# Filler matmuls in the last down product, one combine at its end, and another order of the final norm

## The reference

```python
h2 = rms_norm(x, norm_ffn[l])
for e in range(N_EXPERTS):                       # 32 experts, two chosen per token
    a = jax.nn.silu(hf @ w_gate[e]) * (hf @ w_up[e])
    out = out + combine[:, e:e + 1] * (a @ w_down[e]).astype(f32)
x = x + out
return rms_norm(x, norm_final)                   # y = x * rsqrt(mean(x*x) + EPS) * g
```

## Time and profile before

| | us |
|---|---|
| runs | 728.23, 729.10, 728.98 |
| profiled execution, its own time | 728.23 |
| its span | 726.3 |
| TensorE busy (matmul) | 554.2 (76%) |
| DVE, ACT, POOL busy | 204.1, 72.6, 43.9 |
| weights and other reads | 240.86 MB |

### The profile page before, as it was taken

How to read it: one execution, slowest core, us unless ns; L and a number is a source line. 1 busy time by engine, 2 the same in 40 slices (tenths; PEclk the granted TensorE clock), 3 DMA queues, 4 the chain that set the end, 5 groups by cost and what they waited for, 6 DMA issues and landing times.

```text
span 726.3 us, 7579 instructions
## 1 busy us (share of the span) xinstructions
PE 554.2 (76%) x3257; PEld 331.3 (46%) x3257; DVE 204.1 (28%) x432; ACT 72.6 (10%) x139; POOL 43.9 (6%) x68
## 2 busy tenths in 40 slices
PE   6999999999999998998384594566448347457765
PEld 6888888888886656354041141123114113112411
DVE  3898979897012144000010000000001001000002
ACT  3101020202100013100000000000000000000002
POOL 5001212212000011000000000000000000000000
PEclk9999999999999999999696788779679669778988
DMA  9992812445495648899999999999999999999993
GB/s 248 390 304 83 292 56 71 161 157 192 144 406 232 231 174 319 354 431 428 427 426 430 428 426 430 429 427 426 431 425 427 430 429 427 427 429 426 424 406 152
DMA packets 46097, 242.43 MB, mean 334 GB/s; under 512 B 9618, under 2 KB 9710, under 8 KB 35822
## 3 DMA queue, kind: packets, MB, share of 16 engines
q1 hardware_dynamic: 45198, 238.77, 81.2%
q10 hardware_dynamic: 864, 3.15, 1.3%
HBM read 240.86 MB, written 1.05 MB: 333 GB/s over the span
## 4 chain that ended last, share of the span: by engine, by line
PE 52%; DMA 42%; DVE 2%; SPq 2%; issue 2%; ACT 0%; POOL 0%; DVEq 0%; PEldq 0%; POOLq 0%; ACTq 0%
PE bank L1150 29%; DMA ring<-in_w_down 15%; DMA ring<-in_w_gate 13%; PE bank L1389 8%; DMA s_region<-in_w_up 4%; DMA x_region<-in_w_up 4%; PE bank L1397 4%; DMA ring<-in_w_up 4%; PE bank L1271 4%; PE bank L1438 2%; DMA ring<-in_w_in 1%; SPq L471 1%; PE bank L1356 1%; PE bank L1243 1%; PE bank L1258 1%
## 5 line engine op out<-in xcount | busy, mean ns | idle before, releaser
L1389 PE MATMUL bank<-ring,z_region 128*32 128x512 f32 x688 | 116.3, 668 | 64.0 <-DMA ring<-in_w_gate 14.9
L1150 PE MATMUL bank<-x_region,ring 128*128 128x256 f32 x688 | 152.9, 381 | 0.0
L1150 PEld LDWEIGHTS bank<-x_region,ring 128*128 128x128 f32 x688 | 129.3, 190 | 22.5 <-issue 4.3
L1389 PEld LDWEIGHTS bank<-ring,z_region 128*32 128x32 f32 x688 | 32.8, 121 | 123.5 <-issue 123.5
L1397 PE MATMUL bank<-ring,m_region 128*32 128x512 f32 x240 | 55.4, 737 | 27.8 <-DMA ring<-in_w_down 16.6
L1063 DVE TENSOR_TENSOR z_region<-z_region,bank 128x512 f32<-128x512 f32 x8 | 8.2, 1027 | 209.3 <-PE bank L1389 197.2
L1389 PE MATMUL bank<-x_region,z_region 128*32 128x512 f32 x80 | 43.7, 708 | 11.0 <-DMA ring<-in_w_up 11.0
L1067 DVE COPY m_region<-bank 128x512 f32<-128x512 f32 x8 | 5.5, 692 | 141.7 <-PE bank L1397 113.6
L1397 PE MATMUL bank<-s_region,m_region 128*32 128x512 f32 x64 | 37.3, 750 | 9.0 <-DMA ring<-in_w_down 9.0
L1389 PE MATMUL bank<-rot_region,z_region 128*32 128x512 f32 x64 | 36.0, 727 | 8.4 <-DMA ring<-in_w_up 8.4
L1356 PE MATMUL bank<-conv_region,h_region 128*128 128x128 f32 x256 | 33.2, 285 | 4.7 <-issue 4.1
(11 more groups left out here) (244 smaller groups left out, 551.7 us busy)
## 6 DMA issues: line engine op xcount, KB each, us to landing
ring<-in_w_gate SPq DMA_DIRECT2D x29, 2048.0 KB, 34.5
ring<-in_w_up SPq DMA_DIRECT2D x20, 2048.0 KB, 32.4
ring<-in_w_down SPq DMA_DIRECT2D x20, 2048.0 KB, 35.2
ring<-in_w_in SPq DMA_DIRECT2D x11, 2048.0 KB, 10.3
s_region<-in_w_up SPq DMA_DIRECT2D x4, 2048.0 KB, 34.5
rot_region<-in_w_down SPq DMA_DIRECT2D x4, 2048.0 KB, 32.6
s_region<-in_w_down SPq DMA_DIRECT2D x4, 2048.0 KB, 35.9
x_region<-in_w_up SPq DMA_DIRECT2D x4, 2048.0 KB, 37.0
```

Of the source, the lines that this page charges most:

```text
L1150: ins = MM(dst, w[:, k, n * P:(n + 1) * P], rhs[:, k, :], start=k == 0, stop=k == kn - 1)
L1389: ins = MM(bank[to][quarter(e), :], xT[:, k, quarter(e)], of_expert[e][:, FF * k:FF * k + FF], start=k == 0, stop=k == KD - 1)
```

## The change

In last_down nine fillers are put behind each of the three row units and five behind the first half unit. The combine product between the halves is taken out, and the usual combine(0, PACKS), now with moe_psum on each product, follows the second half; last_down's own three products go.

On DVE the left halves of both blocks and now also the right half of block 1 are multiplied by the gain (times_gain(1, 1), after the fourth combine). The mean of a row is an addition of the two halves' sums and then one scaling with EPS, the second linked to the first by a wait. The order is mean of block 0, wait for its factor, right half of block 0 from the bank; then mean of block 1, wait for its factor, and its right half scaled in place in o_sb. On ACT the last square waits for the third fg_ready.

```diff
-                if h == 0:
-                    act.wait_ge(fg_ready, 2)
+                act.wait_ge(fg_ready, 2 + h)
                 square(1, h)
...
-            def left_mean(b):
-                V.tensor_scalar(stat[:, b:b + 1], stat[:, 6 + 2 * b:7 + 2 * b], 1.0 / D, EPS, ALU.mult, ALU.add).then_inc(left_ready, 1)
             def row_mean(b):
-                V.tensor_scalar(stat[:, 2 + b:3 + b], stat[:, 7 + 2 * b:8 + 2 * b], 1.0 / D, stat[:, b:b + 1],
-                                ALU.mult, ALU.add).then_inc(meansq, 1)
+                link(V.tensor_tensor(stat[:, b:b + 1], stat[:, 6 + 2 * b:7 + 2 * b], stat[:, 7 + 2 * b:8 + 2 * b], ALU.add))
+                V.tensor_scalar(stat[:, 2 + b:3 + b], stat[:, b:b + 1], 1.0 / D, EPS, ALU.mult, ALU.add).then_inc(meansq, 1)
...
-            for b in range(TB):
-                dve.wait_ge(moe_psum, b + 1)
-                times_gain(b, 0)
-            for b in range(TB):
-                dve.wait_ge(sumsq, 4 + 1 + b)
-                left_mean(b)
-            dve.wait_ge(left_ready, TB)
-            for b in range(TB):
-                dve.wait_ge(sumsq, 4 + 3 + b)
-                row_mean(b)
-            for b in range(TB):
-                dve.wait_ge(rstd, 3 + b)
-                scaled_right(b)
+            dve.wait_ge(moe_psum, 1)
+            times_gain(0, 0)
+            dve.wait_ge(moe_psum, 2)
+            times_gain(1, 0)
+            dve.wait_ge(moe_psum, 4)
+            times_gain(1, 1)
+            dve.wait_ge(sumsq, 4 + 3)
+            row_mean(0)
+            dve.wait_ge(rstd, 3)
+            V.scalar_tensor_tensor(o_sb[:, 0, 512:D], bank[1][:], stat[:, 4:5], g_fin[:, 512:D],
+                                   ALU.mult, ALU.mult).then_inc(out_dve, 1)
+            dve.wait_ge(sumsq, 4 + 4)
+            row_mean(1)
+            dve.wait_ge(rstd, 4)
+            V.tensor_scalar(o_sb[:, 1, 512:D], o_sb[:, 1, 512:D], stat[:, 5:6], None, ALU.mult).then_inc(out_dve, 1)
...
-            def combine(o, done):
+            def combine(o, done, last=False):
                 for h in range(2):
                     pe.wait_ge((y_act, y_dve)[h][o], done)
                     for b in range(TB):
...
+                        if last:
+                            ins.then_inc(moe_psum, 1)
...
             def last_down():
                 for c in range(KF - 1):
                     down_rows(0, c, expert_view(expert_loaded(first + c), D))
+                    keep_clock(4, 9)
                 for h in range(2):
...
                     if h == 0:
-                        pe.wait_ge(y_act[0], PACKS)
-                        combine_part(0, 0)
-                combine_part(0, 1)
-                pe.wait_ge(y_dve[0], PACKS)
-                combine_part(1, 0)
-                combine_part(1, 1)
+                        keep_clock(4, 5)
...
             last_down()
+            combine(0, PACKS, last=True)
```

More of the change, by code:

```diff
@@ L321, in block_kernel @@
         fg_ready = sem("fg_ready")
-        left_ready = sem("left_ready")
         out_act = sem("out_act")
@@ L1099, in times_gain @@
                 V.tensor_tensor(o_sb[:, b, half], bank[2 * b + h][:], g_fin[:, half], ALU.mult).then_inc(fg_ready, 1)
-            def scaled_right(b):
-                V.scalar_tensor_tensor(o_sb[:, b, 512:D], bank[2 * b + 1][:], stat[:, 4 + b:5 + b], g_fin[:, 512:D],
-                                       ALU.mult, ALU.mult).then_inc(out_dve, 1)
-            for b in range(TB):
-                dve.wait_ge(moe_psum, b + 1)
-                times_gain(b, 0)
-            for b in range(TB):
-                dve.wait_ge(sumsq, 4 + 1 + b)
-                left_mean(b)
-            dve.wait_ge(left_ready, TB)
-            for b in range(TB):
-                dve.wait_ge(sumsq, 4 + 3 + b)
-                row_mean(b)
-            for b in range(TB):
-                dve.wait_ge(rstd, 3 + b)
-                scaled_right(b)
+            dve.wait_ge(moe_psum, 1)
[13 more added lines that the diff above has]
+            V.tensor_scalar(o_sb[:, 1, 512:D], o_sb[:, 1, 512:D], stat[:, 5:6], None, ALU.mult).then_inc(out_dve, 1)
         @block.tensor
@@ L1381, in combine @@
                     for b in range(TB):
-                        MM(bank[2 * b + h][:], wselT[:, b, :], y_sb[:, 512 * h:512 * h + 512],
-                           start=False, stop=True, skip_group_check=True)
+                        ins = MM(bank[2 * b + h][:], wselT[:, b, :], y_sb[:, 512 * h:512 * h + 512],
+                                 start=False, stop=True, skip_group_check=True)
+                        if last:
+                            ins.then_inc(moe_psum, 1)
             def whole_gate_up(o, done, to, of_expert):
@@ L1464, in down_rows @@
                     ins.then_inc(expert_units, 1)
[L1466 to L1469, removed]
             def last_down():
```

## The result

The changed kernel took 734.55 us (median of four runs, 733.96 to 735.85) against 728.88 us before (728.23 to 729.10): +5.7 us, where the forecast was 735.2 and +6.25. Over all runs of the two kernels the ratio is 1.0105 (95% interval 1.0083 to 1.0127), +7.7 us (+6.0 to +9.3); on a second chip it was 1.0124 (1.0110 to 1.0139), +9.0 us, with a median of 737.96. So it is slower, by what was forecast or up to 3 us more. The four runs of the first median are on the low side of the 25 that the ratio uses (733.96 to 739.18, median 736.03). The changed kernel's runs also lie further apart: 17 of 19 of the kernel before on the second chip lie between 727.75 and 729.95, the other two at 731.72 and 732.64.

What follows compares the result with a forecast made beforehand. TensorE had 52% of the chain of waits and DMA 42%; the end waited for the last half unit of w_down. Fillers 4.49 + tail 2.36 - landing 0.60 = +6.25 us, so 735.2 us, range 733.3 to 736.9.

Steps and rivals of the forecast that it cites:

- The fillers' own price: TensorE's row units and first half: 32 fillers make the last half unit start at 720.25 instead of 715.76, 4.49 us late.
- Rival (a): Row and half units: late weights make TensorE wait anyway, hiding the fillers; only the tail counts, 730.7 us; chance 0.06.
- All combines behind the last half: TensorE after the last half: four combine products take 3.67 us; the fourth ends 4.67 us after the half's start, not 3.87.
- The tail: Last half's start to second output's issue: a second round of mean, power and scaling, 9.17 us instead of 6.81, +2.36.
- Rival (b): End on DVE and ACT: the tail costs nothing and only the fillers count, 732.9 us; chance 0.05.
- The landing: Output DMA: the second output, issued 1.84 us after the first, is alone and lands in 2.7 us, giving 0.6 us back.
- Rival (c): End of the kernel: landing no shorter and tail at upper bound, or the clock falls there: +7.0 to 8.5 us; chance 0.06.
- the 2.15 us of waits: TensorE's waits from first row unit to last half unit, taken as already counted in the fillers' 4.49 us.
- Rival (d): Row units to combines: waits let the clock fall in timed runs and fillers hold it, 7.0 us saved, 728.3; chance 0.02.

Runs made afterwards that it cites:

- e5: The changed kernel, but DVE makes the mean of block 1 before it waits for block 0's factor: 1.0110 to the kernel before, +8.0 us.
- e10: The changed kernel with 30 fillers in the wait for the last up units and six more in the waits for DVE and ACT: 1.0078 to the kernel before, +5.7 us.
- e1: The kernel before with only the 32 fillers added, its combine product between the halves and tail kept: 1.0074 to the kernel before, +5.4 us.
- e2: The changed kernel without its 32 fillers: 1.0038 to the kernel before, +2.8 us.
- e4: The kernel before with only the combine product moved behind the last half, no fillers, norm order as before: 1.0019 to the kernel before, +1.4 us.
- e3: The kernel before with only the new order of the last norm on DVE and ACT: 1.0015 to the kernel before, +1.1 us.
- e7: The changed kernel with 14 fillers (4, 4, 4 and 2) instead of 32: 1.0038 to the kernel before, +2.8 us.
- e9: The changed kernel with 30 more fillers while TensorE waits for the last up units: 1.0081 to the kernel before, +5.9 us.
- e11: The kernel before with 36 fillers in its waits ahead of the row units: 1.0004 to the kernel before, +0.3 us.
- e6: The kernel before with eight fillers, as many as its waits seemed to hold: 1.0029 to the kernel before, +2.1 us.
- e8: The kernel before with DVE's first gain product ahead of its copy of y: 0.9998 to the kernel before, -0.1 us.

## Why the prediction was right, and what it missed

**The fillers' own price: right.** Row to half was forecast at 718.03 + 1.00 + 1.22 - 705.85 = 14.40 us and is 14.48 or 14.49 in four profiles (two of the changed kernel, e5 and e10); the five fillers took 722.41 - 721.10 = 1.31 where the share of nine gave 1.22. Alone they cost 5.4 us (e1). Rival (a), that they are hidden, is refuted by e1 and e2.

**All combines behind the last half: right.** 3.70 us for 3.67; alone 0.67 us in the profile of e4.

**The tail: right in kind, 0.35 us too long.** The second round of mean, power and scaling is there (e3: 7.98 against 6.81, e5). Half to second output was put at 9.17 us and is 8.82. The first output goes out at 7.15 instead of 7.33: DVE starts the addition 0.61 us after the gain product's start, though that is 0.69 long (the two records overlap), and from addition to scaling it is 1.01 us instead of 1.09. The second round saves as much again in the same two ways (0.66 us from the scaling's start to the addition, then 1.02). From the last scaling to the issue it is the 0.77 us forecast, though DVE's in-place scaling takes only 0.48: ACT's takes 0.72 and ends last. Rival (b), a free tail, is out.

**The landing: this step failed, and two misses cancelled.** 0.6 us was to come back, on the argument that the second output, issued later, is alone and lands in 2.7 us as the first does. It doesn't: the first output lands 2.7 us after its issue, so at 1.67 us apart the two still overlap. The second took 3.1 and 3.2 us in the two profiles of the changed kernel, and 3.3 to 3.7 in the five others with the same 1.67 us (e2, e3, e7, e9, e10); 0.64 us apart it took 3.3 in all six. The span's rest behind the second issue fell from 3.73 to 3.57 and 3.55 in the changed kernel, but it is 4.08 in e2, so the term is worth nothing that these profiles can tell. What it gave back too much, about 0.4 us, is by luck what the tail was too long.

Together, from the first row unit to the end: forecast +6.25, measured +6.4.

**Rival (c)** put +7.0 to 8.5 for an unchanged landing with the tail at its upper bound, or for a clock that falls in the tail. By their times the first chip's +7.7 lies in it and the second's +9.0 above it, but its mechanism isn't there: the tail was shorter than forecast, and the clock was 1.00 to the last combine in both profiles of the changed kernel.

**What the sum left out: the room of the kernel before was read from one execution, and the start of the row units is not a constant.** The step said that the 2.15 us of waits were "already counted, as the new sum simply has neither". That is so for the profiled execution, where the row units started early (705.85). From the start of the up product to the first row unit the profiles show 9.63 to 12.55 us, by how much of the up product ran at 1.2 GHz (its sixteen passes start within 6.4 us in e9 and e11, within 9.4 in e1 and e6), and the first row unit with what follows then took 1.6 us more in three of the fourteen profiles (e1, e6, e9). In a kernel that afterwards waits for weights this costs little or nothing: from up to half it is 21.05 us in the kernel before, 20.37 in e2, 21.03 in e3, 20.42 in e4, 20.67 in e8 and 21.65 in e11, though the row unit starts anywhere from 9.65 to 12.12 us behind the up product in them. With 32 fillers there is no wait left, and all of it is paid: 25.52 us from up to half in the changed kernel, 25.98 on the second chip, 29.51 in e1 with its combine product. That is the term that the sum put at nothing. So the fillers cost 25.52 - 21.05 = 4.5 us in a good execution and, by e1's profile without the 0.88 us of its product, 29.51 - 0.88 - 21.05 = 7.6 in a bad one, an estimate from single executions (it belongs to the slowest of e1's five runs, 736.97 against 734.08 to 734.74).

How much of the rest between +6.4 and +7.7 or +9.0 this makes is open. For it: e11 found nothing in the kernel before, and by their times e9 and e10 came out 2 to 3 us under the changed kernel though they have more fillers. Against it: those times are from another chip, and in their profiles the last half unit comes no earlier behind the up product (25.74 and 25.84 us; 25.39 in e5); the spread of e10 was not narrower; and e2, in which TensorE does wait for weights, also took 1 us more than its theory. No profile has the changed kernel with both the up product and the first row unit at full clock. The rival that the programs with the new order reach the up product later (0.9 us on average, see the table) is not excluded either.

Rival (d) had the right part, the clock, with the wrong sign: the clock does fall in some runs near the stretch, at its first row unit, but the fillers stand behind that place, and they took away the waits that made such a fall harmless. So it does not help the changed kernel. The section "HAM oscillation — how this bites in real kernels" of "TensorE: Matmul & The Clock Gate" in the Trainium skill describes matmuls that wait for memory and start cold; the up product does so here in twelve of fourteen profiles (0.93 to 1.03 us a pass at its start, 0.59 in e9 and e11), and fillers can cure it, but by e11 the kernel before gains nothing by that. So of the rule the cold start agrees with these traces, and no gain from curing it is shown in a kernel bound by its loads.

## What to carry to other kernels

Filler matmuls are free only in waits that every execution has; price them by their pitch in the same kernel (here 0.24 us each). If they are to hold the clock, they belong ahead of the place where it falls and not behind it; but no version here became faster by them. Where a late landing decides the end, the waits ahead of it are the cushion that swallows what the engine loses elsewhere; work that fills them adds its own length and the loss that was hidden, so take the start of the stretch from several profiles before the sum. Per-row chains (sum, power, scaling) that are independent should be begun for all rows before the first is finished: a second round behind the first scaling cost 1.2 us in e3's profile, though taking it out of the changed kernel (e5) gave no gain that the runs could tell. And a later issue of the second output is no gain at its landing by itself: 1.67 us apart instead of 0.64 gave none that shows here.

## What was not expected of the hardware

The granted clock fell to 1.2 GHz in a row unit ahead of which TensorE had stood only 1.2 us for DVE and 0.7 us for ACT (e1, e6, and e9, there behind 7 us of fillers and an up product at full clock), and in the nine other profiles with the same two waits it did not. And in e10 it was 1.00 through the 3.09 us of standing after the last filler, only to fall when the product had begun (columns as in e1's stretches):

```profile
692.00:694.00 2.00, 0.26 (x3) 0.07 (x1) 0.00 (x0) 0.00 (x0) 0.00 (x0) 1.00 0.95 389
694.00:695.00 1.00, 0.00 (x0) 0.00 (x0) 0.00 (x0) 0.00 (x0) 0.00 (x0) 1.00 1.02 410
695.00:696.00 1.00, 0.65 (x4) 0.19 (x8) 0.00 (x0) 0.00 (x0) 0.00 (x0) 0.74 1.01 401
696.00:697.00 1.00, 1.00 (x10) 0.34 (x6) 0.00 (x0) 0.00 (x0) 0.00 (x0) 0.50 1.02 406
```
